# A gated DeltaNet and pooling layer on one core: scratch for single transfers, gates and triangular matrices one tile ahead, gate products behind the scan steps, out tile 1 ahead

## The reference

```
h = rms_norm(x) * (1 + scale) + shift            # adaLN from c
u_a, z_a, qkv, z_b, b_raw, a_raw = split(h @ w_in)
y_a = pool_mix(u_a) * silu(z_a)                  # windows 2/4/8/16, then a 128x128 product
q, k, v = silu(causal_conv(qkv))                 # 4 taps; q, k l2-normalised
beta = sigmoid(b_raw);  g = -exp(a_log) * softplus(a_raw + dt_bias)
for chunk:                                       # delta rule, 4 heads of 128
    A = I + strict_lower(beta k k^T * decay);  u, w = solve(A, [beta v, beta k exp(g)])
    v_new = u - w S;  o = q exp(g) S + (q k^T * decay) v_new
    S = S * exp(g_last) + k_decayed^T v_new
y_b = rms_norm(o) * silu(z_b)
y = x + gate * rms_norm(concat(y_a, y_b) @ w_out)
```

## Time and profile before

| | us |
|---|---|
| three runs | 1295.74, 1297.35 (median), 1301.8 |
| the profiled execution's own time | 1301.59 |
| its span, first to last instruction | 1299.8 |
| from the first projection matmul of block 0, 1, 2, 3 to the next | 303.0, 277.2, 280.5, then 360.0 to the end |

### The profile page before, as it was taken

The page is one execution under the profiler, slowest core; times in us unless marked ns, Lnnn a source line. Parts: engine busy times, 40 slices in busy tenths (PEclk is TensorE's granted clock), DMA queues, the critical chain, the costliest instruction groups (busy, mean ns, idle before and its releaser), DMA issues. The chain is left out here.

```text
span 1299.8 us, 17536 instructions
## 1 busy us (share of the span) xinstructions
PE 1188.0 (91%) x6636; PEld 961.8 (74%) x6636; DVE 608.7 (47%) x1220; ACT 364.2 (28%) x714; POOL 218.8 (17%) x225
## 2 busy tenths in 40 slices
PE   5889985999899979998999979998999989999893
PEld 1348864887787868886878868887878879888672
DVE  1256662454425653455346543545245553444524
ACT  2325431223443420113314311123325420111101
POOL 0043241445410010321000010320000001321000
PEclk9889987999899999999999989999999987999997
DMA  8367444443476443213555432213673331221334
GB/s 343 160 217 253 156 153 136 146 146 136 164 283 235 178 126 127 98 66 130 204 217 211 153 115 98 98 66 146 220 273 119 138 114 55 76 97 66 124 138 152
DMA packets 69382, 199.26 MB, mean 153 GB/s; under 512 B 34578, under 2 KB 35858, under 8 KB 52020
## 3 DMA queue, kind: packets, MB, share of 16 engines
q1 hardware_dynamic: 69300, 198.15, 42.5%
HBM read 151.78 MB, written 46.35 MB: 152 GB/s over the span
## 5 line engine op out<-in xcount | busy, mean ns | idle before, releaser
L1829 PE MATMUL acc<-hhi,wsl 128*128 128x512 f32 x768 | 324.3, 422 | 0.8 <-DVE gpw L1093 0.8
L1831 PE MATMUL acc<-hhi,wsl 128*128 128x512 f32 x768 | 305.9, 398 | 0.0
L1830 PE MATMUL acc<-hlo,wsl 128*128 128x512 f32 x768 | 305.8, 398 | 0.0
L1831 PEld LDWEIGHTS acc<-hhi,wsl 128*128 128x128 f32 x768 | 147.8, 193 | 33.6
L1829 PEld LDWEIGHTS acc<-hhi,wsl 128*128 128x128 f32 x768 | 148.7, 194 | 31.2 <-DVE gpw L1093 2.4
L1830 PEld LDWEIGHTS acc<-hlo,wsl 128*128 128x128 f32 x768 | 148.8, 194 | 26.6 <-issue 1.0
L1106 DVE SCALAR_TENSOR_TENSOR cacc<-raw,cw,cacc 128x512 f32<-128x512 f32 x144 | 123.4, 857 | 5.1
L1648 POOL TENSOR_TENSOR wsl<-wraw,wsl 128x512 fp32r<-128x512 f32 x64 | 88.0, 1395 | 192.2 <-ACT wsl L831 192.2
L847 ACT ACTIVATE raw<-acc 128x512 f32<-128x512 f32 x48 | 28.7, 598 | 232.3 <-PE acc L1831 227.4
L1103 DVE TENSOR_SCALAR cacc<-raw,cw 128x512 f32<-128x512 f32 x48 | 23.4, 487 | 133.4 <-ACT cq L894 120.3
L1869 PEld LDWEIGHTS ring<-xv,lt 128*128 128x128 f32 (+1 forms) x384 | 44.3, 180 | 44.5 <-DVE xv L1188 29.0
(11 more groups left out here) (293 smaller groups left out, 1910.0 us busy)
## 6 DMA issues: line engine op xcount, KB each, us to landing
wsl<-kept_w SPq DMA_DIRECT2D x96, 1024.0 KB, 4.8
kept_w<-wsl SPq DMA_DIRECT2D x32, 1024.0 KB, 5.6
wraw<-in_w SPq DMA_DIRECT2D x64, 256.0 KB, 3.4
wada<-in_w_ada SPq DMA_DIRECT2D x6, 2048.0 KB, 16.3
xb<-in_x SPq DMA_DIRECT2D x16, 512.0 KB, 5.7
xres<-in_x SPq DMA_DIRECT2D x16, 512.0 KB, 5.7
out_y<-ytok SPq DMA_DIRECT2D x16, 512.0 KB, 8.2
ssm<-in_s_ssm SPq DMA_DIRECT2D x1, 2048.0 KB, 10.8
```

Source lines behind the costliest of these rows:

```text
L1829: nc.tensor.matmul(acc[t % 2][:], w[:, 0, k], hi[:, k], start=(k == 0), stop=False)
L1830: nc.tensor.matmul(acc[t % 2][:], w[:, 0, k], lo[:, k], start=False, stop=False)
L1831: last = nc.tensor.matmul(acc[t % 2][:], w[:, 1, k], hi[:, k], start=False, stop=(k == KT - 1))
```

## The change

1. **Scratch for single transfers.** `lt` goes out whole, 512-byte rows, one transfer per chunk (`rows_out`); `lb` comes back in one transfer of 16x16 blocks cut out of it; `yx` comes back in one transfer of 4096 pieces of 64 bytes in place of 16 transfers of 256 such pieces. SP issues the inverses at t = `SUB_AT` + 2, in block 0 at t = 15 (16 before).
2. **One tile ahead.** `silu_sq` is of tile t - 1, `SUMS`, the gate steps from the softplus on, `GB_AT`, `EXP_AT`, `KK_AT`, `LT_AT` and `SUB_AT` are each one less.
3. **Gate products behind the scan steps.** `zmul` and the second multiplication (`gated`) stand at the end of the slot; the pooling product stands behind the last part of its z tile, not before it.
4. **Out tile 1 ahead** of `ot` of chunk 3; the high parts of y tiles 0 and 1 are made one slot earlier; out tile 2 waits for the last columns only where it reads them.
5. The decode tokens' spread of the gates (`sb`, `gvb`) moves from before slot 0 to its end.

```diff
@@ -53,7 +53,7 @@
 LAST_PART = NC * NPREP + 3
 FRONT = NC * NPREP - 2
 GATES = 1
-SUMS = 3
+SUMS = 2
 RAW = 3
 BANKS = 6
 WS = 3
@@ -62,11 +62,11 @@
 
 TILES = [("z", 0), ("z", 1), ("z", 2), ("z", 3), ("u", 0), ("u", 1), ("u", 2), ("z", 4), ("u", 3), ("z", 5), ("z", 6), ("z", 7)]
 POOLED_AT = {48: 0, 56: 1, 64: 2, 80: 3}
-GB_AT = {5: (0, 1), 6: (2, 3)}
-EXP_AT = {6: (0, 1), 7: (2, 3)}
-KK_AT = {6: (0, 1), 8: (2, 3)}
-LT_AT = {7: (0, 1), 8: (2, 3)}
-SUB_AT = 10
+GB_AT = {4: (0, 1), 5: (2, 3)}
+EXP_AT = {5: (0, 1), 6: (2, 3)}
+KK_AT = {5: (0, 1), 7: (2, 3)}
+LT_AT = {6: (0, 1), 7: (2, 3)}
+SUB_AT = 9
...
@@ -133,13 +133,13 @@
 
 def pool_after(n):
 
-    if n >= PARTS or n % 8 != 6:
+    if n >= PARTS or n % 8 != 7:
         return None
     kind, z = TILES[n // 8]
     return z - 4 if kind == "z" and z >= 4 else None
...
@@ -428,8 +427,11 @@
         xs, pw8, gr8, ys = (over(n, rd, (16 + 4 * j) * KB, [NS, DM]) for j, n in enumerate(("xs", "pw8", "gr8", "ys")))
 
         kept = nc.dram_tensor("kept_w", (NW, P, 2 * DM), F32, kind="Internal").ap()
-        ltd = nc.dram_tensor("lt_blocks", (NBK, NC * H, BS, BS), F32, kind="Internal").ap()
-        xtd = nc.dram_tensor("inverse_blocks", (NBK, NC * H, 2, BS, BS), F32, kind="Internal").ap()
+        ltd = nc.dram_tensor("lt_rows", (NC * H, P + 1, C), F32, kind="Internal").ap()
+        xtd = nc.dram_tensor("inverse_blocks", (2, P, BS * BS), F32, kind="Internal").ap()
+        lt_blocks = ltd.rearrange("n r i -> (n r i)").rearrange("(q x) -> q x", q=P)[:, 0:BS * C].rearrange(
+            "q (m i) -> q m i", m=BS)[:, :, 0:BS]
+        inverse_rows = xtd.rearrange("e q x -> (e q x)").rearrange("(g p i) -> p g i", p=P, i=BS)
 
         def md(c):
 
@@ -689,25 +691,24 @@
                     sp.wait_ge(*yr_f(it, t))
                     sp.dma_start(a["y"][it, t], ytok[:, t]).then_inc(y_out.sem, 16)
 
-            def blocks_out(it):
-
-                sp.wait_ge(*lt_f(it, NC - 1))
-                for b in range(NBK):
-                    rows = slice(b * BS, (b + 1) * BS)
-                    sp.dma_start(ltd[b].rearrange("n m i -> m n i"), lt[rows, :, :, rows].rearrange("p c h i -> p (c h) i")
-                                 ).then_inc(lt_out, 16)
-                sp.wait_ge(lt_out, 16 * NBK * (it + 1))
+            def rows_out(it, chunks):
+
+                for c in chunks:
+                    sp.wait_ge(*lt_f(it, c))
+                    sp.dma_start(ltd[c * H:(c + 1) * H, 0:P].rearrange("h p i -> p h i"), lt[:, c]).then_inc(lt_out, 16)
+
+            def blocks_back(it):
+
+                sp.wait_ge(lt_out, 16 * NC * (it + 1))
                 sp.wait_ge(*job["pool"](it, -1))
-                sp.dma_start(lb[:], ltd.rearrange("b n m i -> (b n) m i")).then_inc(lb_in, 16)
-
-            def blocks_in(it):
+                sp.dma_start(lb[:], lt_blocks).then_inc(lb_in, 16)
+
+            def inverses(it):
 
                 sp.wait_ge(*sub_f(it, SUBS - 1))
-                sp.dma_start(xtd.rearrange("b n e j i -> (b n) e j i"), xtn[:]).then_inc(x_out, 16)
+                sp.dma_start(xtd.rearrange("e q x -> q e x"), xtn[:].rearrange("p e j i -> p e (j i)")).then_inc(x_out, 16)
                 sp.wait_ge(x_out, 16 * (it + 1))
-                for b in range(NBK):
-                    for e in range(2):
-                        sp.dma_start(yx[b * BS:(b + 1) * BS, e], xtd[b][:, e].rearrange("n j i -> j n i")).then_inc(yx_in, 16)
+                sp.dma_start(yx[:].rearrange("p e n i -> p (e n) i"), inverse_rows).then_inc(yx_in, 16)
 
             for n in range(WR):
                 raw_half(n)
@@ -734,10 +735,14 @@
                         load_tile(it + 1, t + WS - NW)
                     if t == 1 and it:
                         y_rows(it - 1)
-                    if t == SUB_AT - (2 if it else -3):
-                        blocks_out(it)
-                    if t == SUB_AT + (1 if it else 6):
-                        blocks_in(it)
+                    at = t if it else t - 4
+                    if at == 7:
+                        rows_out(it, (0, 1))
+                    if at == 8:
+                        rows_out(it, (2, 3))
+                        blocks_back(it)
+                    if at == SUB_AT + 2:
+                        inverses(it)
                     if 4 <= t < 8 and not last:
 
                         sp.dma_start(xb[:, t - 4], a["x"][it + 1][:, t - 4]).then_inc(x_in.sem, 16)
...
                         sample_tile(it, t)
-                    if t >= 2:
-                        silu_sq(it, t - 2)
+                    if t >= 1:
+                        silu_sq(it, t - 1)
                     if t == GATES + 1:
...
+                        if sc == NC - 1:
+                            act.wait_ge(*job["ks"](it, NC - 1))
+                            for m in range(2):
+                                split_y(it, m)
                     if q == 2 and sc is not None:
...
                         ch = split_step(slot)
                         act.wait_ge(*yb_f(it, ch))
                         split_cols(slice(ch * C, (ch + 1) * C))
-                        if ch == NC - 2:
-                            act.wait_ge(*job["ks"](it, NC - 1))
-                            for m in range(2):
-                                split_y(it, m)
                     if last and slot == SAMPLE_SLOT["conv"]:
...
 
+            def gated(it, t):
+
+                zmul(it, t)
+                g = tile_kind(t)[1] - 4
+                if g >= 0:
+                    dve.wait_ge(*job["pool"](it, g))
+                    dve.wait_ge(*z_f(it, 4 + g))
+                    nc.vector.scalar_tensor_tensor(out=y32[:, g], in0=bank("pool", g)[:], scalar=vec[:, PSC + g:PSC + g + 1],
+                                                   in1=y32[:, g], op0=ALU.mult, op1=ALU.mult).then_inc(ya_f.sem, 1)
+
             def block_of(it, last=False):
...
@@ -1382,7 +1399,7 @@
                         dve.wait_ge(*g_t(it, 0))
                         dve.wait_ge(*b_f(it, -1))
                         nc.vector.tensor_scalar(beta[:], btt[:], 0.5, 0.5, ALU.mult, ALU.add).then_inc(g_b.sem, 1)
-                    if t == GATES + 3:
+                    if t == GATES + 2:
                         dve.wait_ge(*g_l(it, 0))
                         dve.wait_ge(*g_y(it, 0))
                         nc.vector.scalar_tensor_tensor(out=gsp[:], in0=ga[:], scalar=0.0, in1=gl1[:], op0=ALU.max,
...
                             split_y(it, m)
+                    for n in parts:
+                        t = NQ + n // 8
+                        if n < PARTS and n % 8 == 7 and tile_kind(t)[0] == "z":
+                            gated(it, t)
                     if last:
...
                 for j in range(2):
                     k = 2 * kp + j
                     if hf == 0:
-                        pe.wait_ge(*ylo_f(it, k if k < 4 else 5))
+                        pe.wait_ge(*ylo_f(it, min(k, 4)))
                     w_hi_k, w_lo_k = (wsl[:, slot(it, t), e].rearrange("p k c -> p (k c)")[:, j * BT:(j + 1) * BT]
                                       for e in range(2))
                     for tt in range(4):
                         cols = slice(tt * P, (tt + 1) * P)
+                        if hf == 0 and k >= 4 and tt == 3:
+                            pe.wait_ge(*ylo_f(it, 5))
                         if k == 0:
                             if tt >= 2:
                                 bank_free(pe, it, "out", 2 * hf + tt - 2)
...
                         else:
+                            if sc == NC - 1:
+
+                                out_tile(it, 1)
                             turn(it, "ot", sc, lambda h: ao[:, sc % 2, h], (o_s, sc))
                             if sc == NC - 1:
-
-                                out_tile(it, 1)
                                 if last:
                                     sample_out(it, 0)
                                     sample_out(it, 1)
```

More of the change, by code:

```diff
@@ L139, in pool_after @@
     return z - 4 if kind == "z" and z >= 4 else None
-SAMPLE_SLOT = {"conv": 1, "square": 2, "sums": 4, "root": 5, "delta": 6, "rows": 8, "mean": 8, "joined": 30, "gate": 30, "pool": 30,
+SAMPLE_SLOT = {"spread": 0, "conv": 1, "square": 2, "sums": 4, "root": 5, "delta": 6, "rows": 8, "mean": 8, "joined": 30, "gate": 30, "pool": 30,
                "pooled": 31, "mixed": 31}
@@ L166, in psum_jobs @@
             jobs.append(("gt", 0))
-        if t == GATES + 4:
+        if t == GATES + 3:
             jobs.append(("gc", 0))
@@ L203, in psum_jobs @@
                 jobs += [("so", 0), ("sp", OUT), ("sp", OUT + 1)]
-        jobs += {"joined": [("sc", OUT // 4 - 1)], "sums": [("s2", 0), ("kv", 0)], "rows": [("dt", 0), ("son", 0)], "pooled": [("spl", 0)]}.get(
-            next((n for n, at in SAMPLE_SLOT.items() if at == slot and n in ("joined", "sums", "rows", "pooled")), None), [])
```

(30 more changed lines are left out.)

12 lines of the change are left out of this document (5 added, 7 removed).

## The result

The changed kernel takes 1251.8 us (median of four runs, 1250.4 to 1252.4) against 1298.1 for the kernel before in the same session (1295.7 to 1301.8): ratio 0.9639, 95% interval 0.9614 to 0.9664. The prediction was 1251. The profiled execution has a span of 1250.6 us, 49.2 less than before, and a mean granted clock of 0.966 (0.951 before). The medians differ by 46.3: the profile of before is of a slower execution (1301.6), that of the changed kernel of one close to its median (1252.4).

What follows compares the result with a forecast made beforehand. PE was taken to set the time (busy 1188.0 of 1299.8 us), with waits costing again through slow clock behind them. Gains and one loss summed to 45.8 off 1301.6, giving 1255.8, less 4.2: 1251 us, range 1238 to 1270.

Steps and rivals of the forecast that it cites:

- A: Gates and `lt` one tile ahead: PE's waits for `gg` and `lt` and slow clock behind them go, 12.3 us.
- B: silu one tile ahead, substitution before the last two convolutions: wait for the last silu mostly goes, 8.5 us.
- C: Inverses earlier, `yx` in one transfer: `w`'s waits for `xv` nearly go in blocks 1 and 2, shrink in block 0; 20.7 us.
- D: `sb` of the last block behind slot 0: its 4.9 us wait and 3.4 of slow clock go, 8.3 us.
- E: Gate products behind the scan steps: four products' waits with no releaser named go, 5.6 us.
- F: Out tile 1 ahead of `ot`: covers the `ao` waits but uncovers waits for `xn` and `krow`, a loss of 9.6 us.
- out tile 0 starts 1.1 earlier: Block ends, reordered out tiles: out tile 0 starts 1.1 us earlier and runs straight into tile 1, placing `ot` at 617.5.
- (1): Rival: single transfers of small pieces are slower than their summed engine time, `yx` 9.6 us; 1270 us, chance 0.14.
- (4): Rival: pieces of one transfer are fetched one after the other on each engine; 1348 us, chance 0.03.
- (2): Rival: ACT and DVE are coupled, late convolutions hold up copies PE needs, worst in block 0; 1263 us, chance 0.13.
- (3): Rival: out tile 1 ahead of `ot` gains, because `xn` is made earlier than read; 1224 us, chance 0.05.
- (5): Rival: waits are only relabelled, since another chain ends as late everywhere; 1297 us, chance 0.03.

Runs made afterwards that it cites:

- experiment 6: Changed kernel with gates, `lt`, silu, sums and substitution one tile later again, single transfers kept: 1278.0 us against 1300.5 for the kernel before.
- experiment 4: Kernel before with only out tile 1 moved ahead of the `ot` transposes: 1313.6 us against 1297.7, ratio 1.0117.
- experiment 7: Kernel before with only the new scratch layout and single transfers, substitution at its old tile: 1283.8 us against 1300.5, ratio 0.9866.
- Experiment 9: Changed kernel with SP's step of the inverses one step earlier in block 0 alone: 1241.2 us against 1298.6 for the kernel before.
- experiment 8: Changed kernel with gate products ahead of the scan steps again and the pooling product one slot earlier: 1263.4 us against 1300.5 for the kernel before.
- experiment 2: Changed kernel with out tile 1 behind the `ot` transposes again, all else kept: 1236.5 us, 14.9 faster than the changed kernel run again.
- experiment 3: Changed kernel with DVE making `xn` (last block: `krow`) ahead of its wait for `ot`: 1227.1 us, 24.4 faster than the changed kernel run again.

## Why the prediction was right

Span against span, the forecast was 45.8 us less, the measurement is 49.2. The saving of 4.2 taken off for the median was 0.6 (1250.6 + 1.8 around the span against 1251.8). The two nearly cancel, so that the sum came out within 1 us is partly luck. The idle time was forecast as 33.5 us (A 5.5, B 6.0, C 15.5, D 4.9, E 5.6, F 15 - 19 = -4) and is 31.5; the clock as 12.3 and is 17.7.

The table sets the parts side by side. "At its places" is read from the two profiles: the waits named with the result, plus PE's busy time x (1 - PEclk) in the slow stretches behind them. "Undone" is what the changed kernel loses without the part.

| part | forecast | at its places | undone |
|---|---|---|---|
| A | 12.3 | 5.5 + 6.8 = 12.3 | A and B together 23, give or take 4 |
| B | 8.5 | 4.1 + 0.8 = 4.9 | |
| C | 20.7 | 17.1 + 5.2 = 22.3 | 29, give or take 3 (`yx` alone) |
| D | 8.3 | 4.9 + 3.4 = 8.3 | 0, give or take 4 |
| E | 5.6 | 7.1 + 1.7 = 8.8 | 10, give or take 4 |
| F | -9.6 | -7.2 - 2.5 = -9.7 | -15, give or take 3 |
| elsewhere | 0 | 0 + 2.3 | |

The two last columns differ because the parts share one chain: a wait that one edit removes would have been moved or shortened by another. By what undoing shows, D was too high by 8, C too low by about as much, E too low and F's loss too small. That these errors cancel in the sum is luck.

- **A and B** (12.3 + 8.5). Together 23 by experiment 6, which also holds the tile's lead of the inverses. Part of that lead belongs to C. A's waits are all gone. Of B, block 0 keeps 3.3 us and not 1.4, at the place that was named (two convolutions stand behind the substitution there), and 1.6 of the slow clock behind it stayed too. The other 1.9 is the substitution, which takes 9.5 us in block 0 where the prediction had 7.5 (read in block 1): with the tile's lead it runs beside POOL's split of two weight halves, and two of its instructions end with POOL's. It is so in every kernel that has the lead (9.5 to 9.7), and not in the four without (7.5: before and experiments 4, 6 and 7).
- **C** (20.7). The mechanism, its two halves and the places held, but the edit's worth depends on what stands in front of it: 17 us for the transfers alone in the kernel before, 29 for `yx` in the changed one. Forecast and found for `w` of block 0: start at 190 and 191.1, wait 10.9 and 7.9, inverses leaving at 181.2 and 182.8. PE itself came 3.8 us later than I had it (183.2, not 179.4), by the 1.9 of the silu wait and the 1.6 of slow clock behind it, so the shorter wait is B's shortfall and no gain. Blocks 1 and 2 keep 1.2 each, not 0.5; the write of the inverses took 5.7 there where I had 4. `yx` landed in 4.1 where I took 4.7. The Trainium skill, "DMA: Bandwidth & Descriptors", section "Anatomy of one DMA — SWDGE (gpsimd) path", fits about 2.0 us plus bytes over 436 GB/s for DMAs that GpSimd issues, as an estimate 2.6 us for these 256 KB. Here SP issues the DMA, in pieces of 64 bytes, and 4.1 were measured, so that fit does not carry over. Experiment 9 shows that the rest of block 0's wait was SP's queue alone.
- **D** (8.3). The wait went, but D was paid for twice: 2.9 of its 4.9 us go without it, and undoing D alone costs nothing that can be measured.
- **E** (5.6). Too small: 10 by experiment 8, give or take 4. I had priced the four unnamed waits at `w` and given out tile 0's (3.6 us) to F. They are E's. The slow clock behind both was not priced at all (PE's busy time is 7.9 higher in experiment 8's profile, which is of an execution 4.3 above its median; by the median it is 3 to 4), and the new wait of `ks` 2 (2.1), whose bank now hangs on the later gate product, was not seen.
- **F** (-9.6). Sign, places and lengths right: three waits of 4.9 and one of 3.9 where about 5 and 4 were forecast. The size was off: -14.9 in the changed kernel, -15.9 in the one before, where 8.7 are left for the clock and not 5.6. The step that failed is "out tile 0 starts 1.1 earlier" (3.6 us in four blocks), which E does. And in the changed kernel the wait for `ao` would be 8.8 (experiment 2), so F had less to gain than 11.4.

The rivals: (1) is refuted by the landing of 4.1, (4) by the same row. (2), a coupling of ACT and DVE, is no more than the 3.3 us at the last silu; no new wait appeared inside tiles 2 to 11. What (2) said of DVE beside POOL in block 0 is there, at 2.0 us. (3) is refuted by experiments 2 and 4, yet its price of 1224 was fair: with `xn` made earlier (experiment 3) the kernel takes 1227. (5) falls with the result. The column "at its places" divides the clock's gain by where it fell, not by what caused it; the falls move with every shift, and no run isolates one.
